# A hybrid decoder layer: VectorE's squares and first convolution block placed sooner, gelu's argument behind the keys, mem's weight parts split first, all stores by SyncE

## The chip, the cores and the metric

The kernel runs on one core of a Trainium2 chip. Its engines are TensorE (PE, matrix products into PSUM), VectorE (DVE), ScalarE (ACT), GpSimd (POOL) and SyncE (SP), which here only issues transfers. Each engine works through its own instruction list in order and waits on semaphores that others raise. Times are device microseconds of an execution; the metric is their median.

## The reference

One layer on 256 tokens of width 1024, all float32. A pre-norm feeds one input projection with three head groups: stick-breaking attention (8 heads of 64), a recurrent block (RG-LRU, 256 channels, width-4 causal convolution, gelu gate) and cross-attention of 4 heads to 256 memory tokens. Each group is normalised and projected out, and a mixture of 64 experts (8 per token) and one shared expert follow:

```python
h = rms_norm(x, norm_mix_g); proj = h @ w_in
q_sb, k_sb, v_sb, x_rg, gate_rg, q_ca = jnp.split(proj, IN_SPLITS, axis=-1)
o_sb = stick_breaking_attention(q_sb, k_sb, v_sb)
xc = causal_depthwise_conv(x_rg, conv_w, conv_b)
o_rg = gelu(gate_rg) * rg_lru(xc, ...)         # r, i = sigmoid(xc @ w + b); a = exp(..r); scan
o_ca = memory_cross_attention(q_ca, mem, ...)  # rms_norm per head of q and k, softmax
y = concatenate([rms_norm(o_sb), rms_norm(o_rg), rms_norm(o_ca)]) @ w_out
x = x + y
x = x + moe_ffn(rms_norm(x), ...)              # sigmoid router, group-limited top 8, SwiGLU experts
```

## The kernel before

All engines' lists are written by hand. The front part, up to the output projection, follows one common list called `walk`, a sequence of pairs (kind, number). Every engine runs through the same `walk` and picks the kinds in which it has a part, so moving an entry moves it on all engines that take part. Its kinds:

- `unit n`: one block of the input projections or of what follows, made by TensorE in PSUM bank n modulo 4 and copied out by the engine in `owner[n]`. Units 0 to 7 are queries and keys, 8 and 9 the values, 10 and 11 the cross-attention queries, 12 and 13 mem's keys and values, 14 and 15 the recurrent input (into `xpad`), 16 and 17 the gate, 18 and 19 the transposed cross-attention queries and keys (copied to `qkca`), 20 and 21 the two recurrent gates (from the convolution's result `xc`; ScalarE applies the sigmoids), 22 to 25 the cross-attention scores. A unit waits until the unit four before it has been copied out.
- `split_u n`, `split_w n`, `split_a n`: a float32 operand is split into a high and a low part, which are multiplied separately. ScalarE casts the high part, VectorE subtracts it to get the low part. `split_u` is a block of weights for unit n (128x1024), `split_w` 2 and 3 are the two halves of mem's key and value weights (128x2048 each, tile `w_kv`), which unit 12 needs first. TensorE waits for the low part.
- `z h`, `t h`, `av h`: stick-breaking head h. TensorE makes scores for two heads at a time, ScalarE two sigmoids (`beta`, `keep`), GpSimd four causal masks on them (line 650), VectorE two scans and two products (lines 1099 to 1106), TensorE three transposes (`t`, line 1596), ScalarE a copy, TensorE the product with the values (`av`), and VectorE a copy to `yT`. The sigmoids of head h also wait for the transposes of head h - 2, whose buffer they overwrite.
- `ca_square`, `ca_norm`: VectorE squares and sums the cross-attention queries and keys, ScalarE takes a root, VectorE scales.
- `conv`: VectorE's convolution of two channel blocks, four operations each.
- `gelu`: on VectorE gelu's argument in three operations; on ScalarE the squares and gains of the first three blocks of `yT`.

After `walk`, TensorE makes the output projection (line 1637) mixed with the cross-attention, ScalarE the gate's sigmoid, the recurrence's tanh and exponentials and then the softmax exponentials (line 836), VectorE the maxima, the recurrence and the residual sums. The router follows, and VectorE orders the experts and writes their numbers (`ids`, line 1331).

SyncE issues all loads, in a fixed order; weights of 64 experts pass through 22 buffers (cells). The first 6 experts are fixed and some are loaded during the front part. For all others SyncE waits for `ids` (line 554) before it can address them. Then it waits, for each load, for the matmuls that used the buffer last. The results are copied from PSUM to `res`, tile 0 by ScalarE and tile 1 by VectorE, in two halves of 512 columns. `store` on SyncE issues three of the four stores, in the order (tile 0, half 0), (tile 1, half 0), (tile 1, half 1); `store_second` on ScalarE issues the store of tile 0, half 1.

Of the kernel before, what the change touches and what calls it, by code (L numbers as in the profile page):

```python
# [5 lines left out]
def hybrid_decoder_layer(  # L6
# [11 lines left out]
    ALU = mybir.AluOpType  # L18
    ACT = mybir.ActivationFunctionType
    AX = mybir.AxisListType  # L20

    P = 128
    _, SEQ, D = x.shape
    NT = SEQ // P
    KD = D // P
# [27 lines left out]
    for i, kind in enumerate(kinds):  # L53
# [4 lines left out]
        n = {"single": 1, "pair": 2, "fixed": 2, "quad": 4}[kind]  # L58
# [127 lines left out]
    res = at("res", o_A, [P, NT, D])  # L186
# [35 lines left out]
    xc = at("xc", o_V + 8 * KB, [P, 2, SEQ])  # L222
# [6 lines left out]
    xpad = r("xpad", [P, 2, SEQ + 3])  # L229
# [51 lines left out]
    vec = r("vec", [P, 50])  # L281
# [31 lines left out]
    MIX, MEM, GOUT, CW, CB, BR, BI, LAM, QN, KN, GF = 0, 8, 16, 24, 32, 34, 36, 38, 40, 41, 42  # L313

    with ExitStack() as ctx:
# [45 lines left out]
        walk = [("split_u", 3), ("split_u", 4), ("unit", 0), ("unit", 1), ("unit", 2), ("row", 0), ("split_u", 5), ("unit", 3),  # L361
                ("split_u", 6), ("unit", 4), ("split_u", 7), ("log1p", 0), ("split_w", 0), ("unit", 5),
                ("split_w", 1), ("unit", 6), ("mem_norm", 0), ("unit", 7), ("split_u", 10), ("split_a", 1)]
        for i in range(1, 15):
            walk.append(("unit", 7 + i))
            if i <= 8:
                walk.append(("z", i - 1))
            if 4 <= i <= 11:
                walk.append(("av", i - 4))
            if 3 <= i <= 10:  # L370
                walk.append(("t", i - 3))
            walk += {1: [("split_u", 14)], 2: [("split_w", 2)], 3: [("split_w", 3)], 4: [("split_u", 15), ("split_u", 16)],
                     5: [("split_u", 17)], 7: [("ca_square", 0)], 8: [("ca_norm", 0)], 9: [("conv", 0)],
                     11: [("gelu", 0)]}.get(i, [])


        rg_cols = {14: (0, 0), 15: (0, P), 16: (1, 0), 17: (1, P)}
# [28 lines left out]
        def freed(eng, n):  # L406

            count = owner[:n + 1].count(owner[n])
            eng.wait_ge(unit_act if owner[n] == "act" else unit_dve, count)
# [62 lines left out]
        def _(sp):  # L472
            for i in range(2):
                c = slice(i * KD // 2, (i + 1) * KD // 2)
# [74 lines left out]
            for part, e in loads[3 * FIXED + 2:]:  # L549
# [16 lines left out]
                elif part == "down" and e in groups[-1].experts:  # L566
                    i = cell_of[part, e]
# [3 lines left out]
            for half in range(2):  # L571
                c = slice(half * 512, (half + 1) * 512)
# [6 lines left out]
            def store(n):  # L579
                for half in range(2):  # L580
                    c = slice(half * 512, (half + 1) * 512)
                    for t, sem in ((0, out_act), (1, out_dve)):
                        if (t, half) == (0, 1):
                            continue
                        sp.wait_ge(sem, 2 * n + half + 1)
                        sp.dma_start(out[0, t * P:(t + 1) * P, c], res[:, t, c]).then_inc(stored, 16)

# [99 lines left out]
        def _(act):  # L687
# [142 lines left out]
            for h in range(CA_HEADS):  # L830
# [4 lines left out]
                for t in range(NT):  # L835
                    ins = nc.scalar.activation(ca_p[h % 2][:, t, :], ps[:, (22 + h) % 4, t * SEQ:(t + 1) * SEQ], ACT.Exp,
                                               bias=mx[:, t, h:h + 1], scale=SCALE,
                                               accum_out=stat[:, 8 + 2 * (h % 2) + t:9 + 2 * (h % 2) + t])
# [19 lines left out]
            for t in range(NT):  # L858
# [4 lines left out]
                else:  # L863
                    for half, col in ((0, 12), (1, 1)):
                        c = slice(half * 512, (half + 1) * 512)
# [64 lines left out]
                c = slice(half * 512, (half + 1) * 512)  # L930
                nc.scalar.copy(res[:, 0, c], ps[:, ACC[half], :]).then_inc(out_act, 1)

            def store_second(n):

                act.wait_ge(out_act, 2 * n + 2)
                act.dma_start(out[0, 0:P, 512:], res[:, 0, 512:]).then_inc(stored, 16)

            for g in groups:
                group(g)
            act.wait_ge(residual_ps, 1)  # L940
            for half in range(2):
                result(half, 2 * half + 1)
            store_second(0)
            act.wait_ge(extra_dve, 1)
            n_more = nc.scalar.value_load(n_extra[0:1, 0:1], min_val=0, max_val=NE // 2)
            with nc.scalar.If(n_more > 0):
                with nc.scalar.Fori(0, n_more) as i:
                    extra_pair(i)
                act.wait_ge(stored, 64)
                for half in range(2):  # L950
                    result(half, 4 * n_more + (2 * half + 1))
                store_second(1)

        @block.vector
        def _(dve):
            chain = [0]

            def link(ins):
                chain[0] += 1
                ins.then_inc(dve_chain, 1)  # L960
                dve.wait_ge(dve_chain, chain[0])
# [92 lines left out]
            for t in range(NT):  # L1054
                nc.vector.tensor_scalar(rstd_diag[:, t, :], ident[:], stat[:, 2 + t:3 + t], None, ALU.mult).then_inc(diag_dve, 1)

            def conv():

                freed(dve, 14)
                freed(dve, 15)  # L1060
                for c in range(2):
                    link(nc.vector.tensor_scalar(xc[:, c, :], xpad[:, c, 3:3 + SEQ], vec[:, CW + 6 + c:CW + 7 + c],
                                                 vec[:, CB + c:CB + c + 1], ALU.mult, ALU.add))
                    for tap in range(3):
                        ins = nc.vector.scalar_tensor_tensor(xc[:, c, :], xpad[:, c, tap:tap + SEQ],
                                                             vec[:, CW + 2 * tap + c:CW + 2 * tap + c + 1], xc[:, c, :],
                                                             ALU.mult, ALU.add)
                        if tap < 2:
                            link(ins)
                        else:  # L1070
                            ins.then_inc(conv_dve, 1)

            def gelu_argument():
                freed(dve, 16)
# [5 lines left out]
            for kind, n in walk:  # L1080
                if kind == "unit" and owner[n] == "dve":
                    evac(n)
                elif kind == "split_a":
                    split_a(n)
                elif kind == "split_w":
                    split_w(n)
                elif kind == "split_u":
                    split_u(n)
                elif kind == "mem_norm":
                    mean_eps(4, 4)  # L1090
                    inverse(4, 2)
                elif kind == "z":

                    if n == 0:
                        dve.wait_ge(zeroed, 1)
                    dve.wait_ge(mask_pool, 4 * n + 4)
                    b = n % 2
                    kp, rs = keep[b], rest[b]
                    nc.vector.tensor_tensor_scan(rs[:, 0:P][:, ::-1], kp[:, 0:P][:, ::-1], zeros[:, 0:P], 1.0,
                                                 ALU.mult, ALU.add).then_inc(dve_chain, 1)  # L1100
                    nc.vector.tensor_tensor_scan(rs[:, P + 1:NZ + 1][:, ::-1], kp[:, P:NZ][:, ::-1], zeros[:], 1.0,
                                                 ALU.mult, ALU.add).then_inc(dve_chain, 1)
                    chain[0] += 2
                    dve.wait_ge(dve_chain, chain[0])
                    nc.vector.tensor_tensor(beta[b][:, 0:P], beta[b][:, 0:P], rs[:, 1:P + 1], ALU.mult).then_inc(w_dve, 1)
                    nc.vector.tensor_tensor(beta[b][:, P:NZ], beta[b][:, P:NZ], rs[:, P + 2:NZ + 2],
                                            ALU.mult).then_inc(w_dve, 1)
                elif kind == "av":
                    if n % 2:
                        dve.wait_ge(o_ps, n + 1)  # L1110
                        c = (n // 2) % 2 * SEQ
                        nc.vector.tensor_copy(yT[:, n // 2, :], ps[:, 7, c:c + SEQ]).then_inc(yT_dve, 1)
                elif kind == "conv":
                    conv()
                elif kind == "gelu":
                    gelu_argument()
                elif kind == "log1p":
                    log1p()
                elif kind == "ca_square":

                    for u in range(10, 14):
                        freed(dve, u)
                    link(nc.vector.tensor_tensor(ca_sq[:], ca_raw[:], ca_raw[:], ALU.mult))
                    link(nc.vector.reduce_sum(ca_rs[:].rearrange("p a t h -> p (a t h)"),
                                              ca_sq[:].rearrange("p a t (h d) -> p (a t h) d", d=HD), AX.X))
                    nc.vector.tensor_scalar(ca_rs[:], ca_rs[:], 1.0 / HD, EPS, ALU.mult, ALU.add).then_inc(ca_ss_dve, 1)
                elif kind == "ca_norm":
                    dve.wait_ge(ca_rt_act, 1)
                    link(nc.vector.reciprocal(ca_rs[:], ca_rs[:]))
                    heads = ca_raw[:].rearrange("p a t (h d) -> p (a t h) d", d=HD)  # L1130
                    nc.vector.tensor_tensor(heads, heads, ca_rs[:].rearrange("p a t h -> p (a t h)").unsqueeze(2)
                                            .to_broadcast([P, 2 * NT * CA_HEADS, HD]), ALU.mult).then_inc(ca_rs_dve, 1)
# [873 lines left out]
```

## Time and profile before

| | |
|---|---|
| median of 3 runs | 597.75 us (596.48 to 600.49) |
| profiled execution | 598.2 us, span 596.5 us |
| TensorE busy | 556.0 us (93%) |
| VectorE busy | 209.0 us (35%) |
| ScalarE busy | 159.5 us (27%) |
| GpSimd busy | 23.8 us (4%) |
| HBM read | 225.90 MB, 380 GB/s over the span |
| chain that ended last | PE 77%, DMA 14%, DVE 4%, ACT 2%, issue 2% |

The busy share is an average over stages with different limits: the front part up to about 146 us, in which one engine hands to the next, and the expert part, through which weights stream in. A row of the timeline gives start, length, engine, line, operation, output and input, the count of instructions merged in it, and in brackets how long the engine was idle before and who ended that. A bracket with "issue" means that the profile shows no releaser. The granted clock (PEclk) is a share of 2.4 GHz; 0.50 is 1.2 GHz.

### The profile page before, as it was taken

The page shows a single profiled execution, that of the slowest core. Times are in us where ns is not written, and L with a number is a line of the kernel's source. Part 1 is how long each engine was busy: PE and PEld are TensorE (multiplying, and loading weights), DVE is VectorE, ACT ScalarE, POOL GpSimd, SP SyncE. Part 2 cuts the span into 40 slices and gives each one's busy share as a digit, 9 for nine tenths or more (in the row PEclk, how much of TensorE's full clock was granted, in tenths as well). Part 3 has the DMA queues.
Part 4 walks back from the last instruction along what each step waited for, and adds up shares of the span by engine and source line. Part 5 has one row for each costly group of instructions (what it writes and reads, how often), then busy time and mean ns, then how long its engine had stood idle before and what let it go on. Part 6 is the DMA issues. An engine that isn't in the chain of part 4 may idle for free.

```text
span 596.5 us, 8294 instructions
## 1 busy us (share of the span) xinstructions
PE 556.0 (93%) x3148; PEld 306.2 (51%) x3149; DVE 209.0 (35%) x532; ACT 159.5 (27%) x307; POOL 23.8 (4%) x78
## 2 busy tenths in 40 slices
PE   8998988999999999999999999999988999379994
PEld 6987874456454444445445444454544444124441
DVE  2879596756322522222122222222221222102212
ACT  5785346425211111111011111111110111101112
POOL 1015141000000000000000000000000000000000
PEclk9999999999999999999999999999998999769999
DMA  8996459609999999999999999999999999999993
GB/s 315 419 420 266 170 221 416 271 15 371 407 416 403 423 420 421 421 430 421 429 427 423 422 428 424 422 430 425 424 426 427 431 423 436 426 413 415 413 401 146
DMA packets 26776, 227.50 MB, mean 381 GB/s; under 512 B 3184, under 2 KB 3312, under 8 KB 7664
## 3 DMA queue, kind: packets, MB, share of 16 engines
q1 hardware_dynamic: 26448, 226.67, 91.6%
q8 instruction: 26, 0.43, 0.3%
q10 hardware_dynamic: 288, 0.29, 0.1%
q14 instruction: 14, 0.11, 0.0%
HBM read 225.90 MB, written 1.05 MB: 380 GB/s over the span
## 4 chain that ended last, share of the span: by engine, by line
PE 77%; DMA 14%; DVE 4%; ACT 2%; issue 2%; POOL 1%; SPq 0%; ACTq 0%; POOLq 0%; DVEq 0%
PE ps L1773 30%; PE ps L1802 12%; DMA cell_three<-in_w_e 8%; PE ps L1732 8%; PE ps L1812 7%; DMA cell_two<-in_w_e 4%; PE ps L1637 4%; PE ps L1533 3%; PE ps L1500 3%; PE ps L1514 2%; PE ps L1793 1%; DMA wA<-in_w_qk 1%; PE ps L1779 1%; PE ps L1785 1%; PE ps L1547 1%
## 5 line engine op out<-in xcount | busy, mean ns | idle before, releaser
L1773 PE MATMUL ps<-cell_two,xg 128*64 128x512 f32 (+2 forms) x496 | 110.5, 615 | 18.1 <-DMA cell_three<-in_w_e 13.9
L1802 PE MATMUL ps<-cell_d,e_hT 128*64 128x512 f32 (+2 forms) x440 | 87.6, 597 | 2.2 <-DVE e_hT L1396 1.5
L1773 PE MATMUL ps<-cell_gu,xg 128*64 128x512 f32 (+2 forms) x416 | 78.3, 595 | 0.0
L1393 DVE TENSOR_TENSOR e_h<-e_sg,ps 128x256 f32<-128x256 f32 x28 | 11.8, 421 | 186.2 <-ACT e_sg L899 186.2
L1773 PEld LDWEIGHTS ps<-cell_two,xg 128*64 128x64 f32 (+2 forms) x496 | 34.5, 132 | 82.5 <-issue 82.5
L899 ACT ACTIVATE e_sg<-ps 128x256 f32<-128x256 f32 x28 | 10.7, 384 | 208.5 <-PE ps L1773 208.5
L1451 DVE SCALAR_TENSOR_TENSOR ylo<-ps,gslot,yhi 128x512 fp32r<-128x512 f32 x52 | 39.0, 750 | 72.0 <-ACT yhi L910 72.0
L1732 PE MATMUL ps<-pick,xhi 128*128 128x256 f32 x224 | 58.5, 300 | 0.3 <-DVE pick L1309 0.3
L1732 PE MATMUL ps<-pick,xlo 128*128 128x256 f32 x224 | 54.3, 281 | 0.0
L910 ACT ACTIVATE yhi<-ps,gslot 128x512 fp32r<-128x512 f32 x52 | 35.7, 687 | 69.4 <-PE ps L1802 69.3
L1732 PEld LDWEIGHTS ps<-pick,xhi 128*128 128x128 f32 x224 | 42.2, 188 | 19.1 <-issue 18.8
L1773 PEld LDWEIGHTS ps<-cell_gu,xg 128*64 128x64 f32 (+2 forms) x416 | 25.6, 128 | 47.9 <-issue 47.6
L1802 PEld LDWEIGHTS ps<-cell_d,e_hT 128*64 128x64 f32 (+2 forms) x440 | 25.7, 126 | 40.0 <-issue 39.5
L1812 PE MATMUL ps<-yhi,S 128*128 128x512 f32 x104 | 43.0, 413 | 0.9 <-DVE ylo L1451 0.9
L1732 PEld LDWEIGHTS ps<-pick,xlo 128*128 128x128 f32 x224 | 42.4, 189 | 1.0 <-issue 1.0
L1812 PE MATMUL ps<-ylo,S 128*128 128x512 f32 x104 | 40.9, 393 | 0.0
L1773 PE MATMUL ps<-cell_three,xg 128*64 128x512 f32 (+1 forms) x144 | 38.1, 657 | 0.4 <-DMA cell_three<-in_w_e 0.4
L886 ACT ACTIVATE xg<-ps,vec 128x256 f32<-128x256 f32 x60 | 25.2, 471 | 23.7 <-PE ps L1732 23.6
L1637 PE MATMUL ps<-wo,yT 128*128 128x512 f32 x64 | 29.6, 603 | 0.4 <-DVE x L1176 0.4
L1435 DVE TENSOR_TENSOR xg<-ps,vec 128x512 f32<-128x512 f32 x26 | 18.0, 691 | 30.9 <-PE ps L1732 30.9
L906 ACT CAST S<-ps 128x256 fp32r<-128x256 f32 x26 | 9.7, 372 | 59.8 <-PE ps L1787 59.8
L1390 DVE TENSOR_REDUCE gslot<-ps 64x1 f32<-64x2 f32 (+2 forms) x64 | 10.0, 157 | 42.6 <-ACT S L906 41.4
(336 smaller groups left out, 676.3 us busy)
## 6 DMA issues: line engine op xcount, KB each, us to landing
cell_two<-in_w_e SPq DMA_DIRECT2D x31, 2048.0 KB, 25.3
cell_d<-in_w_e SPq DMA_DIRECT2D x51, 1024.0 KB, 21.5
cell_gu<-in_w_e SPq DMA_DIRECT2D x48, 1024.0 KB, 14.6
cell_three<-in_w_e SPq DMA_DIRECT2D x9, 3072.0 KB, 23.0
wo<-in_w_out SPq DMA_DIRECT2D x1, 4096.0 KB, 12.4
wA<-in_w_qk SPq DMA_DIRECT2D x7, 512.0 KB, 10.9
wR<-in_w_rest SPq DMA_DIRECT2D x3, 1024.0 KB, 28.4
wV<-in_w_v SPq DMA_DIRECT2D x1, 2048.0 KB, 18.8
```

The costliest lines, as they stand in the source:

```text
L886: nc.scalar.mul(rows_of(c, slice(k, k + 1), slice(0, 2)).squeeze(1), ps[:, Y[step % 2], k % 2 * 2 * P:(k % 2 + 1) * 2 * P].rearrange("p (g ...
L910: nc.scalar.mul(yhi[:, half * 512:(half + 1) * 512], ps[:, Y[half], :], gslot[:, g.routed % 2:g.routed % 2 + 1]).then_inc(yhi_act, 1)
L1435: nc.vector.tensor_tensor(rows_of(g.chunk + 1, slice(2 * step, 2 * step + 2), slice(0, 2)), ps[:, Y[1], :].rearrange("p (k g s) -> p k g s ...
L1451: nc.vector.scalar_tensor_tensor(ylo[:, c], ps[:, Y[half], :], gslot[:, g.routed % 2:g.routed % 2 + 1], yhi[:, c].bitcast(F32), ALU.mult, ...
L1500: last = mm(b[:, 0:SEQ], part[:, k, :], a[:, k, :], start=k == 0 and m == 0, stop=k == KD - 1 and m == 2)
L1514: last = mm(b[:, 0:SEQ], w[:, k, c:c + P], hT[:, k, :], start=k == 0, stop=k == KD - 1)
L1533: last = mm(b, a[:, k, c:c + P], w[:, k, :], start=k == 0 and m == 0, stop=k == KD - 1 and m == 2)
L1637: last = mm(ps[:, ACC[2 * t + half], :], yT[:, k, t * P:(t + 1) * P], wo[:, k, half * 512:(half + 1) * 512], start=k == chunks[0], stop=k ...
L1732: last = mm(o, part[:, t, k, :], pick[c % 2][:, t, :], start=i == 0, stop=i == 3)
L1773: last = mm(ps[side * w:(side + 1) * w, U, :], rows(k, slice(side * w, (side + 1) * w)), weight[:, k - k0, :], start=k == 0, stop=k == KD - 1)
L1802: last = mm(ps[side * w:(side + 1) * w, Y[half], :], e_hT[:, kk, side * w:(side + 1) * w], n[:, kk, half * 512:(half + 1) * 512], start=kk ...
L1812: last = mm(ps[:, ACC[2 * t + half], :], to_token[:, t * P:(t + 1) * P], y[:, half * 512:(half + 1) * 512], start=False, stop=sem is not N ...
```

## The change

In `walk`, `split_w` 2 and 3 each come one step sooner, and `split_u` 14, which stood before them, comes behind them. `ca_square` comes one step sooner, behind unit 13 instead of unit 14. `conv` is taken apart: block 0 stands two steps sooner than the whole did, behind unit 14's step, and block 1 where the whole stood. `gelu` stands one step later, behind unit 19 instead of unit 18. On ScalarE this changes nothing in its order, since ScalarE has no part in unit 19; on VectorE the copy of the keys (unit 19) now comes ahead of gelu's argument. All four stores are issued by SyncE, in the order (0,0), (1,0), (0,1), (1,1) of (tile, half), and ScalarE's store is gone.

```diff
@@ walk
-            walk += {1: [("split_u", 14)], 2: [("split_w", 2)], 3: [("split_w", 3)], 4: [("split_u", 15), ("split_u", 16)],
-                     5: [("split_u", 17)], 7: [("ca_square", 0)], 8: [("ca_norm", 0)], 9: [("conv", 0)],
-                     11: [("gelu", 0)]}.get(i, [])
+            walk += {1: [("split_w", 2)], 2: [("split_w", 3)], 3: [("split_u", 14)], 4: [("split_u", 15), ("split_u", 16)],
+                     5: [("split_u", 17)], 6: [("ca_square", 0)], 7: [("conv", 0)], 8: [("ca_norm", 0)], 9: [("conv", 1)],
+                     12: [("gelu", 0)]}.get(i, [])
@@ SyncE, store
-                        if (t, half) == (0, 1):
-                            continue
@@ ScalarE
-            def store_second(n):
-
-                act.wait_ge(out_act, 2 * n + 2)
-                act.dma_start(out[0, 0:P, 512:], res[:, 0, 512:]).then_inc(stored, 16)
...
-            store_second(0)
...
-                store_second(1)
@@ VectorE
-            def conv():
-
-                freed(dve, 14)
-                freed(dve, 15)
-                for c in range(2):
-                    link(nc.vector.tensor_scalar(xc[:, c, :], xpad[:, c, 3:3 + SEQ], vec[:, CW + 6 + c:CW + 7 + c],
-                                                 vec[:, CB + c:CB + c + 1], ALU.mult, ALU.add))
-                    for tap in range(3):
...
+            def conv(c):
+
+                freed(dve, 14 + c)
+                link(nc.vector.tensor_scalar(xc[:, c, :], xpad[:, c, 3:3 + SEQ], vec[:, CW + 6 + c:CW + 7 + c],
+                                             vec[:, CB + c:CB + c + 1], ALU.mult, ALU.add))
+                for tap in range(3):
+                    ins = nc.vector.scalar_tensor_tensor(xc[:, c, :], xpad[:, c, tap:tap + SEQ],
+                                                         vec[:, CW + 2 * tap + c:CW + 2 * tap + c + 1], xc[:, c, :],
+                                                         ALU.mult, ALU.add)
+                    if tap < 2:
+                        link(ins)
+                    else:
+                        ins.then_inc(conv_dve, 1)
...
                 elif kind == "conv":
-                    conv()
+                    conv(n)
```

## Rows read from the trace of the kernel before

**Rows 1.** Windows: busy us and count per engine, PEclk, DMA share, GB/s.
```profile
120.00:134.00 14.00, 13.57 (x60) 8.02 (x58) 8.10 (x16) 4.05 (x9) 0.00 (x0) 1.00 0.07 12
...
260.00:300.00 40.00, 39.06 (x176) 21.12 (x178) 7.61 (x19) 5.42 (x12) 0.00 (x0) 1.00 1.01 425
```

**Rows 2.** Waits of SyncE's queue: total us, times, longest.
```profile
SPq L554 <- DVE ids L1331: 9.4, 1, 9.4
```

**Rows 3.** Timeline of TensorE, 51 to 98 us.
```profile
51.43 0.49 PE L1596 MATMUL ps<-ident,beta 128*128 128x128 f32 x3
...
88.11 3.36 PE L1547 MATMUL ps<-xc,wg 64*64 64x256 f32 x16 [2.38 <-issue]
...
94.17 2.10 PE L1554 MATMUL ps<-qkca 64*128 64x256 f32 x16
...
97.83 0.60 PE L1560 MATMUL ps<-ones,y_sq 128*128 128x1 f32 x4 [0.50 <-ACT ca_p L836]
```

**Rows 4.** Chain that ended last: start, length, engine, what.
```profile
57.12 3.04 PE ps L1533 x12
```

**Rows 5.** Windows around the two stops of TensorE.
```profile
56.00:57.00 1.00, 0.00 (x0) 0.00 (x0) 1.00 (x2) 0.00 (x0) 0.00 (x0) 1.00 0.00 0
57.20:85.70 28.50, 28.40 (x206) 23.80 (x206) 19.93 (x41) 10.87 (x24) 7.44 (x34) 1.00 0.46 185
...
88.00:89.00 1.00, 0.89 (x5) 0.60 (x7) 1.00 (x4) 0.00 (x0) 0.00 (x0) 0.50 0.36 88
```

**Rows 6.** Issue of mem's weights on SyncE, and their landing.
```profile
11.69 0.43 SPq L486 DMA_DIRECT2D w_kv<-in_w_mem  x1
...
w_kv<-in_w_mem SPq DMA_DIRECT2D x1, 2048.0 KB, 26.7
```

**Rows 7.** Timeline of ScalarE, casts of high parts.
```profile
42.97 1.05 ACT L767 CAST hi_unit<-wR 128x1024 fp32r<-128x1024 f32 x1
...
44.66 1.93 ACT L756 CAST w_kv_hi<-w_kv 128x2048 fp32r<-128x2048 f32 x1
```

**Rows 8.** Timeline of GpSimd, two stretched pairs of masks.
```profile
49.83 2.61 POOL L650 TENSOR_SCALAR_AFFINE_SELECT keep<-keep 128x128 f32<-128x128 f32 x2 [2.08 <-ACT keep L804]
...
77.41 1.52 POOL L650 TENSOR_SCALAR_AFFINE_SELECT keep<-keep 128x128 f32<-128x128 f32 x2 [1.84 <-ACT keep L804]
```

**Rows 9.** Timeline of VectorE, low parts.
```profile
46.30 1.30 DVE L1047 TENSOR_TENSOR wR_lo<-wR,hi_unit 128x1024 fp32r<-128x1024 f32 x1
...
54.69 2.37 DVE L1040 TENSOR_TENSOR w_kv_lo<-w_kv,w_kv_hi 128x2048 fp32r<-128x2048 f32 x1
```

**Rows 10.** Timeline of VectorE, head 6 and the squares.
```profile
75.60 0.42 DVE L1099 TENSOR_TENSOR_SCAN rest<-keep,zeros 128x128 f32<-128x128 f32 x1 [3.34 <-POOL beta L650]
...
77.52 1.25 DVE L1123 TENSOR_TENSOR ca_sq<-ca_raw 128x1024 f32<-128x1024 f32 x1
...
80.14 0.42 DVE L1007 TENSOR_TENSOR xpad<-ps,rstd_row 128x256 f32<-128x256 f32 x1
```

**Rows 11.** Window from head 6's scans to the convolution's end.
```profile
75.60:88.00 12.40, 10.04 (x85) 8.64 (x83) 12.01 (x26) 7.07 (x14) 5.14 (x24) 0.98 0.59 225
```

**Rows 12.** Timeline of ScalarE, sigmoids of the gates to the softmax.
```profile
86.26 1.28 ACT L736 ACT_TABLE_LOAD   x1
90.13 0.47 ACT L736 ACTIVATE rg_r<-ps,vec 128x256 f32<-128x256 f32 x1 [2.58 <-PE ps L1547]
...
91.51 0.47 ACT L736 ACTIVATE rg_i<-ps,vec 128x256 f32<-128x256 f32 x1 [0.40 <-PE ps L1547]
...
96.63 0.45 ACT L836 ACTIVATE ca_p<-ps,mx 128x256 f32<-128x256 f32 x1
```

**Rows 13.** Timeline of the end: stores and last copy.
```profile
590.32 1.77 SPq L586 DMA_DIRECT2D out<-res  x3
...
591.05 0.69 DVE L1464 COPY res<-ps 128x512 f32<-128x512 f32 x1 [0.16 <-PE ps L1812]
591.20 0.36 ACTq L936 DMA_DIRECT2D out<-res  x1
```

More of the change, by code:

```diff
@@ L1055, in _ @@
                 nc.vector.tensor_scalar(rstd_diag[:, t, :], ident[:], stat[:, 2 + t:3 + t], None, ALU.mult).then_inc(diag_dve, 1)
-            def conv():
-                freed(dve, 14)
-                freed(dve, 15)
-                for c in range(2):
-                    link(nc.vector.tensor_scalar(xc[:, c, :], xpad[:, c, 3:3 + SEQ], vec[:, CW + 6 + c:CW + 7 + c],
-                                                 vec[:, CB + c:CB + c + 1], ALU.mult, ALU.add))
-                    for tap in range(3):
[L1065 to L1071, printed above, removed]
+            def conv(c):
[10 more added lines that the diff above has]
+                        ins.then_inc(conv_dve, 1)
             def gelu_argument():
```

## The prediction, made before the changed kernel ran

> **What bounds the kernel now.** I read the windows first. In the expert part the transfers set the pace: 425 GB/s at a share of 1.01, for instance between 260 and 300 us [rows 1]. In the front part they do not: from 120 to 134 us the same engines run at 0.07. So the expert stream is a block of nearly fixed length, and the question is when it starts. The waits of SyncE's queue answer it: its last long wait before the stream, 9.4 us, is for the expert numbers (ids) that VectorE writes at the end of routing [rows 2]. All that routing needs is the chain projections, attention, output projection, router. A microsecond taken off that chain starts the stream a microsecond earlier; one taken off an engine beside it brings nothing.
>
> Then I went down TensorE's timeline for places where this chain stands still. There are two that the edit touches. (1) The second half of unit 12 (mem times its key and value weights) starts at 57.12 [rows 4]; before it TensorE is idle, its clock still granted at 1.00 [rows 5], because VectorE ends the low part of that weight half at 54.69 + 2.37 = 57.06 [rows 9]. (2) Unit 20 (the recurrent gate) starts at 88.11 after 2.38 us of idleness [rows 3], because VectorE's convolution ends only then. Between the two TensorE works 28.40 of 28.5 us [rows 5]. The second stop costs twice: the clock falls to its lower level of 1.2 GHz (0.50 from 88 to 89 us), and the sixteen small matmuls of units 20 and 21 take 3.36 us, where sixteen of the same 64x256 output take 2.10 us at the full 2.4 GHz later on [rows 3].
>
> **Edit 1, mem's weight parts first.** ScalarE casts split_u 14 from 42.97 (1.05 us) and the first mem half only at 44.66 [rows 7]. w_kv is in SBUF by then: SyncE issues it at 11.69 and it lands 26.7 us later [rows 6], at 38.4. Now the mem half is cast from 42.97 to 44.9, and head 1's two sigmoids behind it come 0.9 us later. VectorE subtracts from 46.30 [rows 9], 2.3 us instead of 1.3, so the first low part stands at 48.6. Head 1's scans wait for GpSimd's masks, and those are what this edit endangers: a mask pair that begins together with the 128x2048 subtraction took 2.61 us [rows 8]. Head 1's masks now begin at about 45.8 and VectorE is in that subtraction till 48.6. I take them as held till then. What is left of the 2.61 after the subtraction, 0.3, is about one of the four masks (an estimate), so three or four remaining ones are done by 49.5 to 49.8. A head's scans and products take 1.6 us (75.60 to 77.52 [rows 10], less a copy of 0.3), so they end by 51.1 to 51.4, and the second mem subtraction by 53.8. TensorE asks for head 1 at 51.43 [rows 3] (margin 0.3 to 0.0, so a short wait is possible) and for the second half at about 55.0, when twelve matmuls of unit 12 are through (margin 1.2). Without a stop the second half starts at 51.95 + 3.04 = 54.99 instead of 57.12: **2.1 us off TensorE**, bounds 1.4 (head 1's masks 0.7 later than I think) and 2.4 (all of the idle before 57.12, were the masks early). Queued behind the moved operations: split_u 14, wanted by unit 14 ten microseconds later; head 2's masks, which meet the second subtraction and end 1 to 2 us later than now, wanted by TensorE only after unit 12, at 58. Both have more slack than they lose: 0.
>
> The Trainium skill ("SBUF — State Buffer", section "SBUF: two separate sides") states that GpSimd and VectorE operations with two SBUF inputs take a shared port pair as an exclusive lock for a whole instruction. The trace agrees [rows 8]: 2.61 us is the length of VectorE's subtraction and a little. By that rule this edit is a loss for head 1's masks, of the size I put in; were the engines only to share bandwidth, the masks would be through 1 us sooner and the risk at 51.43 would fall away.
>
> **Edit 2, squares and convolution sooner.** Before head 6's scans VectorE is idle 3.34 us [rows 10]. The squares of cross-attention take from 77.52 to 80.14, 2.6 us [rows 10], and behind unit 13 they fit that gap (their inputs, units 10 to 13, are complete there). From 75.60 to 88.0 VectorE is busy 12.01 of 12.40 us [rows 11]; take 2.6 out of the stretch and move it 2.1 earlier, and the convolution ends at 88.0 - 2.1 - 2.6 = 83.3. TensorE comes to unit 20 at 88.11 - 2.38 - 2.1 = 83.6. The stop is gone, if only just. A charge against it: the first convolution block now lies over head 7's masks. Today the squares do, and the pair took 1.52 [rows 8]. Held to the end of a 1.9 us block, the masks would be some 0.7 us late, the convolution would end at 84.0, TensorE would idle 0.4 us. Splitting the convolution adds no instruction, only one passed semaphore wait: 0. ScalarE's root (ca_norm) gets its input earlier: 0, off the path.
>
> **What follows on ScalarE decides the sum.** Behind unit 20 the path runs through ScalarE: table load from 86.26, sigmoids of unit 20 at 90.13 after an idle of 2.58, of unit 21 at 91.51 after 0.40, and from there without pause to the first softmax exponential at 96.63 [rows 12]; TensorE waits for it at 97.83 [rows 3]. The table load moves with TensorE, to 84.2, and ends at 85.4. Unit 20's result is there at 83.6 + 16/2 matmuls at full clock (0.9) + the 0.3 of drain that 90.13 shows = 84.8, or 85.2 with the late masks. So the table load is last, both idle spans go, and the gain at the exponential is 2.1 + 2.58 + 0.40 = **5.1 us**. It can't be more: TensorE's own gain (2.1 + 2.4 + 1.3 = 5.8) ends in a wait before 97.83 that grows from 0.50 to about 1.2 us. That is shorter than the idle at 56 us, which left the clock alone [rows 5].
>
> **Edit 3, gelu's argument behind the keys.** The same three operations on VectorE, about 1.8 us (an estimate from the 1.25 of one product twice as wide, three times half of that [rows 10]); they end near 87, wanted by ScalarE at 88. The keys' copy comes first instead and TensorE, with two blocks of output projection ahead of the scores, doesn't need it: 0. Cover gone would cost at most those 1.8.
>
> **Edit 4, stores.** SyncE starts its three stores at 590.32 and the third ends at 592.09; ScalarE's was issued at 591.20, for 0.36 us [rows 13]. In SyncE's list it stands before the last, which waits for VectorE's copy till 591.05 + 0.69 = 591.74. SyncE has that half microsecond free: +0.1, at most +0.4. What I can't see is how the four land. 4.4 us pass from the last issue to the end of the span, four 256 KB stores at 425 GB/s need 2.5; a better order could return up to 1.9.
> The Trainium skill ("DMA: Bandwidth & Descriptors", section "Issuing engines are not separate DMA queues") says that issuing from several engines saves only issue time. By that the edit could cost the 0.36 us of an issue and never return anything; the sum goes by the rows.
>
> **Sum.** The profiled execution took 598.2 us, 0.45 above the median of 597.75. 598.2 - 5.1 + 0.1 = 593.2; against the median **592.7**, 0.85% less.
>
> **Rivals.**
> A, chance 0.57: the above, 592.7, with own bounds 591.5 to 594.
> B, 0.20: only the first stop goes for good. Masks held by two-input operations more often than I count make the convolution end after 85, TensorE idles over 1 us and the clock falls as it does today. Then unit 21's sigmoids keep their distance of 3.4 us from the start of unit 20, and the gain is about 88.11 - 85.2 = 2.9: 594.9. For it: margins of 0.3 us at both stops. Against: ScalarE's table load covers 0.6 us of lateness.
> C, 0.11: the sum of A, and the stores land without the 1.9 us tail: 590.8. For it: the unexplained time in rows 13; against: nothing shows that ScalarE's queue causes it.
> D, 0.07: the front part is shorter but the end stays, because the stream's rate or a late fixed transfer sets it: 597.8. Against: the 9.4 us wait for ids, and a share of 0.07 just before [rows 1, 2].
> E, 0.05, the other side: head 1's masks are late by enough to stop TensorE at 51.43, and the clock falls there. One fall costs what rows 3 show, about 1.3 us. Gains of 5.1 are used up when the wait passes 5.1 - 1.3 = 3.8 us, that is masks done past 53. For 600 (2.2 slower) they would have to end near 55.6. Each pair would have to be held for more than 2.61 us, after VectorE has gone idle.
>
> **Numbers.** Two medians of a few runs can tell about 1% (6 us) from no change; by it the border to faster lies at 591.8. A falls below it in 3 of 10 (a gain 0.9 above the sum, or the spread of 4 us seen between three runs), C mostly, B rarely: faster 0.27. Slower than 603.7 needs E at its worst or a mechanism I don't see: 0.04. The rest, 0.69, is within 1%. Range: A and C with the unknown of the tail give 590.3 at the low end; B with 1 us of spread gives 596.3 at the high end; D and E are left out.
>
> **What would show it.** Right: unit 12's second half at about 55.0 without a wait; VectorE's idle before head 6's scans near 1 us; unit 20 near 83.7 with the clock at 1.00 and under 2.2 us for the sixteen matmuls of units 20 and 21; ScalarE's sigmoids directly behind the table load near 85.4; the wait for ids over 5 us sooner than today. Wrong: an idle before head 1's transposes at 51 us, a new 0.50 in the clock, masks ending after 79, or a stream that starts 5 us sooner and yet ends as late as before.

## The result, and the profile after

The changed kernel takes 592.12 us (median of 6 runs, 591.82 to 592.97), against 598.33 for the kernel before in the same runs (596.17 to 600.49). The ratio is 0.9898, 95% interval 0.987 to 0.9926, that is 4.4 to 7.8 us. The forecast was 592.7; its 0.85% less lies inside the interval. The profiled execution took 591.89 us with a span of 590.2.

Neither of TensorE's two stops is left. In its timeline the transposes of head 1 start on time, and unit 20 starts without a bracket. A third wait, the one before the row sums (the last line here), has grown from 0.50 to 1.30 us. The answer to [rows 3] is

```profile
51.16 0.49 PE L1585 MATMUL ps<-ident,beta 128*128 128x128 f32 x3
...
82.64 1.94 PE L1536 MATMUL ps<-xc,wg 64*64 64x256 f32 x16
...
91.75 0.60 PE L1549 MATMUL ps<-ones,y_sq 128*128 128x1 f32 x4 [1.30 <-ACT ca_p L834]
```

In the chain that ended last, unit 12 now stands in one piece ([rows 4] had its second half alone):

```profile
51.66 5.49 PE ps L1522 x24
```

The windows (columns as in [rows 5]) show TensorE busy where the first stop was, and at unit 20 the granted clock at 1.00 where it had been 0.50:

```profile
50.00:56.00 6.00, 6.00 (x35) 5.21 (x34) 5.76 (x8) 3.88 (x6) 4.82 (x8) 1.00 0.69 288
...
83.00:84.00 1.00, 1.00 (x14) 0.62 (x12) 1.00 (x3) 0.98 (x2) 0.00 (x0) 1.00 0.79 203
```

On ScalarE the sigmoids follow the table load directly; the brackets of [rows 12], 2.58 and 0.40, are gone:

```profile
83.25 1.28 ACT L734 ACT_TABLE_LOAD   x1
84.55 0.48 ACT L734 ACTIVATE rg_r<-ps,vec 128x256 f32<-128x256 f32 x1
...
85.43 0.47 ACT L734 ACTIVATE rg_i<-ps,vec 128x256 f32<-128x256 f32 x1
...
90.55 0.46 ACT L834 ACTIVATE ca_p<-ps,mx 128x256 f32<-128x256 f32 x1
```

VectorE's idle time before head 6's scans, 3.34 in [rows 10], is filled by the squares:

```profile
68.84 1.22 DVE L1112 TENSOR_TENSOR ca_sq<-ca_raw 128x1024 f32<-128x1024 f32 x1
...
72.60 0.43 DVE L1088 TENSOR_TENSOR_SCAN rest<-keep,zeros 128x128 f32<-128x128 f32 x1 [0.75 <-POOL beta L648]
```

GpSimd's masks do pay for it, as [rows 8] let expect: the second pair of head 1 (46.22) and the second of head 2 (50.41) each lie under a mem subtraction. The second pair of head 7 (75.03) lies under the first convolution block.

```profile
46.22 2.58 POOL L648 TENSOR_SCALAR_AFFINE_SELECT beta<-beta 128x128 f32<-128x128 f32 x2
...
50.41 2.77 POOL L648 TENSOR_SCALAR_AFFINE_SELECT beta<-beta 128x128 f32<-128x128 f32 x2
...
75.03 1.08 POOL L648 TENSOR_SCALAR_AFFINE_SELECT beta<-beta 128x128 f32<-128x128 f32 x2
```

VectorE writes the expert numbers at 145.14 in the kernel before (first line) and at 139.08 in the changed one (second line):

```profile
145.14 0.21 DVE L1331 CAST ids<-ps 1x58 int32<-1x58 f32 x1
139.08 0.21 DVE L1320 CAST ids<-ps 1x58 int32<-1x58 f32 x1
```

### The profile page after: what moved, and what is told of

It is laid out like the page before. It is cut to its first block, busy times and chain, and to the rows that moved or that the text cites. A ratio compares the mean times of both kernels' runs of the same rounds, so it can differ in the third digit from the quotient of the medians.

```text
span 590.2 us, 8293 instructions
## 1 busy us (share of the span) xinstructions
PE 554.5 (94%) x3148; PEld 305.1 (52%) x3149; DVE 209.2 (35%) x532; ACT 159.5 (27%) x307; POOL 24.3 (4%) x78
## 4 chain that ended last, share of the span: by engine, by line
PE 81%; DMA 10%; DVE 4%; ACT 3%; issue 1%; SPq 0%; DVEq 0%; ACTq 0%
PE ps L1762 32%; PE ps L1791 14%; PE ps L1721 9%; PE ps L1801 7%; DMA cell_two<-in_w_e 5%; DMA cell_three<-in_w_e 4%; PE ps L1626 4%; PE ps L1522 4%; PE ps L1489 3%; PE ps L1503 2%; PE ps L1782 1%; PE ps L1511 1%; PE ps L1768 1%; DMA wA<-in_w_qk 1%; PE ps L1774 1%
```

## The experiments

All are compared through one measure from their profiles: the time from VectorE's first scan of head 0 (44.3 to 45.0 us; in VectorE's list nothing ahead of it was moved) to the writing of `ids`, which starts the stream. Behind the first softmax exponential little moved: from its start to `ids` ten profiles show 48.5 us, two show 50.2 (told below), and softmax_first, which changes the order of the exponentials, 48.7. From `ids` to the start of the last copy of the result all show 444.6 to 446 us. The runs below were made in three sets, each with the kernel before beside it (medians 597.60, 597.93 and 597.35 us; 598.33 beside the changed kernel above); a ratio holds within its set.

The column on the clock tells of the stretch ahead of `ids` alone. Further on, in the expert part, all thirteen profiles show 0.50 in two stretches, between 440 and 454 us and between 508 and 532, and once more at the end.

```
kernel           scan->ids   clock at 0.50 ahead of ids         median us  lowest..highest  ratio [95%]
before             100.52    at unit 20                          (3 sets)   595.32..600.67
changed             94.74    nowhere                             592.12     591.82..592.97   0.9898 [0.987, 0.9926]
mem_only            96.39    nowhere                             594.81     594.45..595.96   0.9955 [0.9939, 0.9971]
vector_only         99.03    at 58 us                            595.24     594.01..596.84   0.9956 [0.994, 0.9973]
clock_held         100.66    at 58 us                            596.70     595.48..597.64   0.9977 [0.9962, 0.9992]
both_held           99.10    nowhere                             596.53     595.44..597.35   0.9978 [0.996, 0.9995]
stores_back         96.36    at 93 us                            592.36     592.02..593.28   0.9906 [0.9886, 0.9926]
squares_back        96.50    nowhere                             593.82     593.70..594.50   0.9938 [0.9915, 0.9962]
conv_whole          94.68    nowhere                             592.06     591.83..592.42   0.9906 [0.9875, 0.9937]
gelu_back           94.70    nowhere                             592.73     590.26..594.82   0.9919 [0.9893, 0.9944]
changed_again       96.42    at 93 us                            592.02     590.62..593.84   0.9907 [0.988, 0.9935]
preload             93.91    nowhere                             590.96     590.42..592.03   0.9894 [0.987, 0.9918]
softmax_first       93.73    nowhere                             591.31     589.82..591.96   0.9896 [0.9871, 0.9921]
```

**mem_only**: edit 1 alone, on the kernel before.

```diff
-            walk += {1: [("split_u", 14)], 2: [("split_w", 2)], 3: [("split_w", 3)], ...
+            walk += {1: [("split_w", 2)], 2: [("split_w", 3)], 3: [("split_u", 14)], ...
```

> Before, with split_w 2 and 3 ahead of split_u 14 and nothing else changed. My theory: VectorE and TensorE behind unit 12 both come about 2.7 us sooner, the idle of 2.4 us before unit 20 stays and with it the fall of the clock, since VectorE's stretch to the convolution's end moves along: total 2.4 to 2.8 us below the kernel before. Rival (the two stops overlap: one VectorE delay seen twice): the idle before unit 20 grows by what unit 12 gains, total unchanged within 0.5 us. Second rival (head 1's masks are held long enough to stop TensorE at 51 us): gain below 1.5 us and an idle before the transposes at 51 us.

The median is 2.8 us below (ratio 0.9955). TensorE's timeline and windows show a surprise:

```profile
85.57 1.94 PE L1547 MATMUL ps<-xc,wg 64*64 64x256 f32 x16 [2.38 <-issue]
```

```profile
84.00:85.00 1.00, 0.00 (x0) 0.00 (x0) 0.93 (x3) 0.99 (x1) 0.15 (x1) 1.00 0.70 222
86.00:87.00 1.00, 1.00 (x13) 0.79 (x10) 1.00 (x3) 0.31 (x1) 0.00 (x0) 1.00 0.44 135
```

The same idle of 2.38 us as in [rows 3], to the hundredth, but no fall of the clock behind it: the sixteen matmuls take 1.94 and not 3.36. So the median is as the theory had it, and one of its parts is not: the idle alone doesn't settle whether the clock falls.

**vector_only**: edits 2 and 3 alone. The diff is that of the change without the order of the splits and without the stores.

> Before, with only VectorE's moves (squares and first convolution block sooner, gelu's argument behind the keys). My theory: unit 12's wait of 1.9 us stays; ScalarE's two idle spans before the sigmoids (2.58 and 0.40 us) go, the clock stays at 1.00 around unit 20: total 3.0 us below before, and the gains of the two parts add up to that of the whole. Rival (only the lateness of the convolution counts, not the clock): 1.6 us or less. Rival (masks of head 7, held by the convolution block, make it late): an idle of over 1 us before unit 20 and a gain under 1.5 us.

2.4 us below before in the medians (2.6 by the ratio). Unit 20's stop is gone and its clock is 1.00, but this time the first stop's idle, which had left the clock alone in [rows 5], was answered:

```profile
56.00:57.00 1.00, 0.00 (x0) 0.00 (x0) 1.00 (x2) 0.00 (x0) 0.00 (x0) 1.00 0.00 0
58.00:59.00 1.00, 1.00 (x5) 0.76 (x4) 0.96 (x4) 0.00 (x0) 0.00 (x0) 0.58 0.00 0
59.00:60.00 1.00, 1.00 (x4) 0.80 (x3) 1.00 (x1) 0.00 (x0) 0.00 (x0) 0.50 0.00 0
60.00:61.00 1.00, 1.00 (x4) 0.71 (x3) 1.00 (x2) 0.00 (x0) 0.00 (x0) 0.50 0.00 0
```

The chain that ended last has the second half of unit 12 as

```profile
57.05 4.57 PE ps L1531 x12
```

Twelve matmuls took 4.57 us there, against the 3.04 of [rows 4]: 1.5 us, about the price at unit 20 (3.36 - 1.94 = 1.4). The executions without a profile have their mean granted clock on record: four of the nine stand at 0.979 or 0.980, the profiled one among them, and take 595.8 to 596.8 us; five stand at 0.982 to 0.985 and take 594.0 to 595.2. That suggests that the fall came in about half of them. It doesn't prove it, since the mean covers the expert part too (mem_only, with no fall ahead of `ids`, has 0.980).

**clock_held**: on the kernel before, work of no use in the second stop, so that TensorE isn't idle.

```diff
                 elif n < 22:
+                    if n == 20:
+                        for _ in range(5):
+                            mm(b[:, 0:SEQ], ident[:], iota1[:, 0:SEQ], start=True, stop=True)
                     pe.wait_ge(conv_dve, 2)
```

> Before, with five 128x256 matmuls of no use put on TensorE ahead of unit 20's wait for the convolution (about 2.2 us, into its idle of 2.38); they add work and take none away. Theory (half of the price of the second stop is the clock that falls in it): unit 20 still starts near 88.1, the granted clock stays at 1.00, the sixteen matmuls take about 1.9 instead of 3.36 us, the sigmoids of unit 21 start 1.3 to 1.5 us sooner and the total is 1.3 to 1.5 us below before. Rival (the clock falls for another reason than the idle, or costs nothing because ScalarE is behind anyway): total unchanged within 0.3 us.

```profile
87.04 2.32 PE L1545 MATMUL ps<-iota,ident 128*128 128x256 f32 x10
89.53 1.94 PE L1551 MATMUL ps<-xc,wg 64*64 64x256 f32 x16 [0.17 <-DVE xc L1065]
```

Work was added and the kernel is faster: 0.9977 [0.9962, 0.9992], 1.4 us by the ratio, as expected, and 0.9 us in the medians. Unit 20's clock is at 1.00, as the mechanism wants it; the profile alone doesn't prove the mechanism, since mem_only kept its clock there without such work. (These times stand 1.5 us later than before's because the first stop's clock fell in this profile, as in vector_only.)

**both_held**: as clock_held, with three such matmuls ahead of unit 12's second half as well, into PSUM bank 1.

```diff
                         for k in range(KD):
+                            if (n, k) == (12, 4):
+                                freed(pe, 9)
+                                for _ in range(3):
+                                    mm(ps[:, 1, 0:SEQ], ident[:], iota1[:, 0:SEQ], start=True, stop=True)
```

> The kernel before, with matmuls of no use in both stops: three ahead of unit 12's second half (1.4 us of the 1.94 idle) and five ahead of unit 20 (2.3 of 2.38). They only add work. Theory (each stop is answered by a clock fall of about 1.5 us in some executions, which is also where the spread of the kernel before comes from): the clock is 1.00 at both places, all executions lie within 1.3 us of each other instead of 4, the median is 1.5 to 2.2 us below before, near 595.7, and the changed kernel is 4.0 to 4.4 below that. Rival (the spread is the transfers'): the spread stays at 2 us and more and the median equals that with one stop filled.

```profile
55.18 1.46 PE L1533 MATMUL ps<-iota,ident 128*128 128x256 f32 x6
```

```profile
58.00:59.00 1.00, 1.00 (x6) 0.78 (x6) 0.96 (x3) 0.00 (x0) 0.00 (x0) 1.00 0.06 16
88.00:89.00 1.00, 0.83 (x9) 0.56 (x10) 1.00 (x3) 0.00 (x0) 0.00 (x0) 1.00 0.82 107
```

Half right. The profile has the clock at 1.00 in both places, and its measure is 1.56 us below that of clock_held, whose first stop was answered by a fall. No execution of either held kernel is above 597.7, while before reaches 600.7. But the median, 596.53, is about that of clock_held (596.70) and not the 595.7 expected, and the executions spread over 1.9 us, not 1.3: the rival's two signs nearly came too. The mean granted clocks give a likely reason for the equal medians. Of clock_held's eleven executions only two, the profiled one and another, stand at 0.979, so for most of them there was no fall left to prevent. In both_held all twelve stand at 0.982 to 0.984, so its 1.9 us have another cause. Of the 52 executions of before in the three sets, the nine at 599.7 us and above stand at 0.977 (eight) or 0.980 (one), and 0.977 appears in no other kernel; that fits falls in both stops at once, which no profile here shows.

**squares_back**, **conv_whole**, **gelu_back**: the changed kernel with one part undone each.

```diff
squares_back
-   5: [("split_u", 17)], 6: [("ca_square", 0)], 7: [("conv", 0)], 8: ...
+   5: [("split_u", 17)], 7: [("ca_square", 0), ("conv", 0)], 8: ...
conv_whole
-   7: [("conv", 0)], 8: [("ca_norm", 0)], 9: [("conv", 1)],
+   8: [("ca_norm", 0)], 9: [("conv", 0), ("conv", 1)],
gelu_back
-   12: [("gelu", 0)]
+   11: [("gelu", 0)]
```

> The changed kernel, with the squares of cross-attention back behind unit 14's step (the convolution stays in two blocks, mem's parts stay first). Theory (the squares are the part that ends the second stop, and an idle of some 2 us is answered by a fall of the clock in some executions only): VectorE idles 3.3 us before head 6's scans again, the convolution ends 2.3 to 2.6 us later, TensorE idles about 2.3 us before unit 20, unit 20's sigmoids come 1.5 us later where the clock stays and unit 21's 2.9 us later where it falls: 1.5 to 2.9 us above the changed kernel, and single executions spread over 1.3 us. Rival (convolution in two blocks is what matters): within 0.3 us of the changed kernel.

> The changed kernel, with both convolution blocks together behind unit 16's step, as before the change. Theory (VectorE's total work to the convolution's end counts, the division hardly): head 7's masks come a pair free, its scans about 1 us sooner, the convolution ends 0.5 to 1 us later, TensorE idles under 1 us before unit 20, and ScalarE's table load hides it: within 0.3 us of the changed kernel. Rival (the block in two is needed to end the second stop): an idle of about 2 us before unit 20, 1 to 2 us slower.

> The changed kernel, with gelu's argument ahead of the keys' copy again, on VectorE. Theory: the keys' copy ends 1.8 us later, near 86, still before TensorE's scores at 87.3 and the argument before ScalarE's use at 87: within 0.2 us of the changed kernel. Rival (the scores or unit 23 wait for the keys): an idle before the scores and 0.5 to 1 us slower.

The squares are the part that counts: undone, the measure rises by 1.8 us (96.50 against 94.74) and the median by 1.8 (593.82 against 592.06 of conv_whole beside it). The lost time doesn't lie in one idle of 2.3 us, though, as expected, but in three short ones, since the scaling (ca_norm) and head 7 are late too:

```profile
PE ps L1529 <- DVE ca_raw L1120: 0.9, 1, 0.9
PE ps L1585 <- DVE beta L1095: 0.9, 1, 0.9
PE ps L1536 <- issue: 0.5, 1, 0.5
```

(waits of TensorE from 40 to 92 us: total, times, longest). The convolution's division is worth nothing: with both blocks together unit 20 waits 0.38 us and ScalarE's table load hides it, 592.06.

```profile
83.24 1.95 PE L1536 MATMUL ps<-xc,wg 64*64 64x256 f32 x16 [0.38 <-issue]
```

Nor is gelu's move: 94.70 against 94.74. Its median is 0.6 above the changed kernel's, with executions from 590.26 to 594.82. Its profile shows no fall ahead of `ids`, but the three executions from 593.94 us up stand at a mean granted clock of 0.979, the three from 591.66 to 592.73, the profiled one among them, at 0.982, and the fastest at 0.984. The two profiles told next, with a fall at the third place, stand at 0.979 as well, so that fall is the likely cause of the slow three.

**stores_back**: the changed kernel with ScalarE's store (`store_second`, and the `continue` on SyncE) as before.

> The changed kernel, with ScalarE's store of tile 0, half 1 put back. Theory (the four stores are worth nothing either way): from the last copy's end to the span's end 4.8 us as in before, instead of 4.9 in the changed kernel; total within 0.3 us of the changed kernel, that is 6.1 us below before. Rival (ScalarE's queue made the late landing): 1 to 2 us slower than the changed kernel, 4 to 5 below before.

592.36 against 592.12: no difference that can be told. From the last copy's end to the end of the span the profiles show 4.76 us in before (591.05 + 0.69 to 596.5), 4.63 here, 4.89 in the changed kernel. Over all thirteen profiles the six with ScalarE's store show 4.10 to 4.76 and the seven without it 4.67 to 5.00, so all four stores on SyncE cost 0.1 to 0.3 us (an estimate, as the two groups overlap). The rival of 1 to 2 us falls. But this profile brought the third place at which the clock can fall, and that one is of the change's own making.

**changed_again**: the changed kernel once more.

> The changed kernel once more, beside the two below. Theory (a stop of TensorE is answered by a fall of the clock in some executions only; this kernel has one stop of 0.8 to 1.3 us left, before the row sums at 92 us): most executions near 592.1, some 1.5 to 1.7 us above, as the one profiled of stores_back. Rival (that profile was a stray one): all within 0.6 us.

```profile
92.28 0.61 PE L1549 MATMUL ps<-ones,y_sq 128*128 128x1 f32 x4 [1.30 <-ACT ca_p L834]
92.75 5.38 PE L1626 MATMUL ps<-wo,yT 128*128 128x512 f32 x8
```

```profile
91.00:92.00 1.00, 0.00 (x0) 0.00 (x0) 0.96 (x3) 0.97 (x4) 0.00 (x0) 1.00 0.97 410
93.00:94.00 1.00, 1.00 (x2) 0.36 (x2) 0.96 (x4) 0.28 (x2) 0.00 (x0) 0.57 1.08 459
94.00:95.00 1.00, 1.00 (x2) 0.34 (x1) 0.96 (x6) 0.00 (x0) 0.00 (x0) 0.50 0.95 401
```

Eight matmuls of the output projection take 5.38 us; with the clock up they take 3.68. Two of the six executions, 593.66 and 593.84, lie 1.7 us above the median of 592.02. The first of them is the profiled one; that the other is of the same kind is argued from its time and its mean granted clock, 0.979 in both against 0.982 to 0.984 in the other four.

**preload** and **softmax_first**: what the profiles pointed to next. The first brings ScalarE's sigmoid table in while ScalarE waits, behind the root of ca_norm; the second also computes two heads' softmax exponentials ahead of the recurrence's.

```diff
preload
                     nc.scalar.activation(ca_rs[:], ca_rs[:], ACT.Sqrt).then_inc(ca_rt_act, 1)
+                    act.wait_ge(act_chain, chain[0])
+                    nc.scalar.activation(stat[:, 14:15], stat[:, 14:15], ACT.Sigmoid).then_inc(act_chain, 1)
+                    chain[0] += 1
softmax_first, in addition
-            for c in range(2):
-                nc.scalar.activation(rg_a[:, c, :], rg_r[:, c, :], ACT.Exp, ...).then_inc(rg_act, 1)
             for h in range(CA_HEADS):
+                if h == 2:
+                    for c in range(2):
+                        nc.scalar.activation(rg_a[:, c, :], rg_r[:, c, :], ACT.Exp, ...).then_inc(rg_act, 1)
```

> The changed kernel, with ScalarE's sigmoid table loaded right behind the root of ca_norm, in ScalarE's idle time before 80 us, by a sigmoid of one column. Theory (behind unit 20 the table load of 1.28 us is last, then the result of unit 20 itself): the table load before unit 20's sigmoids is gone, they start near 83.8 instead of 84.55, unit 21's near 84.8 instead of 85.4, the first exponential and the total come 0.6 us sooner. Rival (TensorE is the bound after all, through the scores): the exponential's gain ends in an idle of VectorE or TensorE and the total stays within 0.2 us.

> preload, and in addition ScalarE computes the softmax exponentials of heads 0 and 1 ahead of the recurrence's two exponentials. Theory: the first exponential comes 1.1 us sooner than in the changed kernel, TensorE's stop before the row sums shrinks to under 0.3 us, VectorE's recurrence product comes 0.6 us later but off the path: total 1.0 us below the changed kernel and executions closer together. Rival (head 0's normalised rows then come too late for TensorE's transposes): a new idle of 0.5 us and more before unit 27 and no gain over preload.

preload's ScalarE, with the sigmoids' table load moved ahead of 80 us, and softmax_first's TensorE:

```profile
76.48 1.28 ACT L810 ACT_TABLE_LOAD   x1
84.09 0.47 ACT L734 ACTIVATE rg_r<-ps,vec 128x256 f32<-128x256 f32 x1 [0.54 <-PE ps L1539]
```

```profile
90.83 0.60 PE L1552 MATMUL ps<-ones,y_sq 128*128 128x1 f32 x4 [0.15 <-ACT ca_p L837]
```

The measure falls by 0.8 and 1.0 us against the changed kernel's 94.74. The wait before the row sums shrinks from 1.30 to 0.52 and 0.15 us, and no fall follows it in either profile. The medians are 590.96 and 591.31 against 592.02 of changed_again beside them, and neither has an execution above 592.1. The 95% intervals overlap that of changed_again, so the medians don't prove a gain, and between the two kernels the runs don't decide. What the timelines show, in one profile of each, is that the front part is shorter by 0.8 to 1.0 us, and where that comes from.

## Why the prediction was right, point by point

- **What bounds** (the stream is a fixed block, its start is what counts): right. `ids` moved from 145.14 to 139.08, 6.1 us, and the span shrank by 6.3. Rival D falls. So does rival B: unit 20 starts without a wait and its clock is at 1.00.
- **Edit 1**: forecast 2.1, measured 2.7 (100.52 - 96.39 for mem_only is 4.1, of which 1.4 are the clock fall that this profile lacks; both_held, also without a fall, gives 99.10 - 96.39 = 2.7). The mechanism was right and the size off: I took the 3.04 us of [rows 4] as the length of twelve matmuls, but it holds the start after a stop; all twenty-four now take 5.49, so twelve take 2.74. The smaller wait before the first half (before's list of waits has 2.2 us for the two, 1.94 for the longer) was left out of the sum. The two make 0.6 us, and the 2.7 lies above my upper bound of 2.4.
- **The masks under the subtraction**: right. Head 1's second pair took 2.58 us, ending at 48.80, 0.4 behind the subtraction that began at 46.03 for 2.38; I had said 49.5 to 49.8. The masks didn't even hold the scans, which begin at 48.98 behind another copy of VectorE's. The scans and products end at 50.73 and TensorE asks at 51.16, so rival E did not come about. Head 2's pair took 2.77 and cost nothing, as said. The Trainium skill ("SBUF — State Buffer", section "SBUF: two separate sides") says that of a GpSimd operation and a VectorE operation with two SBUF inputs the one that starts later is blocked for the whole of the other. The trace agrees with both: a pair that takes 0.54 while VectorE is idle (at 60.88) took 2.58 and 2.77 beside subtractions of 2.38 and 2.37.
- **Edit 2**: forecast 2.58 + 0.40 = 2.98 on ScalarE; measured 3.07 (from table load to unit 21's sigmoid 91.51 - 86.26 = 5.25 before, 85.43 - 83.25 = 2.18 after). That holds only against an execution in which the clock falls at unit 20. Without the fall the distance is 3.85 (mem_only: 83.71 to 87.56), and the edit is worth 1.67. The late masks of head 7 cost less than I feared: TensorE reached unit 20 without a wait. Of the edit's two moves only the squares bring something (squares_back, conv_whole); I gave the division no price of its own.
- **Edit 3**: 0, right. **Edit 4**: +0.1, measured +0.1 to 0.3; rival C falls, ScalarE's queue was not behind the late landing.
- **Wrong**: the clock. I wrote that the new wait before 97.83 "is shorter than the idle at 56 us, which left the clock alone", and so gave it no price, and in rival B that the clock "falls as it does today". One profile can't say that. In these profiles the idle of 1.9 us at 56 us was followed by a fall in two of three, that of 2.4 us before unit 20 in one of two, and that of 1.3 us before the row sums in two of five (stores_back, changed_again; not in changed, gelu_back, vector_only). A second wait of 1.31 us, some 6 us behind the row sums, stands in all thirteen profiles, and no fall follows it in any. Each fall costs 1.4 to 1.7 us (3.36 - 1.94, 4.57 - 3.04, 5.38 - 3.68). In rival E I had put 1.3, from sixteen matmuls of another unit that take 2.10 at the higher clock, where these take 1.94.
- **The sum**: the stops alone, without falls, are worth 99.10 - 94.74 = 4.36 us (2.71 + 1.65). The median fell by 6.2 and, in the last set, by 5.3. The rest, 1 to 2 us, fits what the falls at two places gave back, less what the third now costs: both_held, which only prevents falls, is 1.3 us below before by its ratio. In the pair of profiles, one with the fall at unit 20 and one without, the sum closes: 2.71 + 3.07 = 5.78 = 100.52 - 94.74. My 5.1 had a stop too small by 0.6 and a fall counted as certain. Over many executions the two errors partly cancel, and so the closeness of the total is in part luck.

## What to carry to other kernels

Fill an engine's idle gap with work that stands in front of the late result, and first look at which other engine is last behind it: here a table load of 1.28 us covered 0.38 us of lateness and made one part of the change worthless, and moving that load shortened the front part by 0.8 us in its profile. Price a stop of TensorE twice, its length and, with some chance, 1.5 us of low clock behind it; don't take that chance from one profile. When one engine gets ahead, note the wait that grows further on: here it went from 0.50 to 1.30 us, and the clock fell behind it in two of the five profiles that have it.

## What the runs showed of the hardware

The granted clock's answer to the same idle differs from execution to execution: 2.38 us before unit 20 led to 0.50 in one profile and left 1.00 in another, 1.30 us before the row sums led to 0.50 in two of five, and 1.31 us some 6 us later never did, in thirteen. With five matmuls of no use in the gap before unit 20 the clock stayed at 1.00 there in both profiles that have them, and the kernel with these alone was 1.4 us faster by its ratio. What decides between the outcomes was not tried, and stays open, as does the spread of 1.9 us in both_held.
